# A 528-column product finishes its first 264 columns before it starts the second

## The reference

```python
def hybrid_layer(x, norm_g, w_in, q_norm_g, k_norm_g, rpb, w_o_attn, w_o_na, w_out, cos, sin):
    h = rms_norm_2(x, norm_g)
    proj = jnp.einsum('bld,de->ble', h, w_in)
    qa, ka, va, za, qb, kb, vb, zb, ga, gb = split_cols(proj)
...
    ya = jnp.einsum('ble,ed->bld', oa, w_o_attn)
    yb = jnp.einsum('ble,ed->bld', ob, w_o_na)
    mixed = jax.nn.sigmoid(ga) * ya + jax.nn.sigmoid(gb) * yb
    return x + jnp.einsum('bld,de->ble', mixed, w_out)
```

## Time and profile before

| | |
|---|---|
| median of 3 runs | 1615.57 us (1615.27 to 1616.48) |
| the profiled execution | 1616.05 us |
| its span, first to last instruction | 1614.8 us |
| mean granted TensorE clock | 0.994 |
| PE, PEld, DVE, ACT busy | 96%, 83%, 55%, 39% |
| line 581 (all matmuls of `pe_terms`) on the chain that ended last | 69% of the span |

### The profile page before, as it was taken

How to read it: one execution, slowest core, us unless ns; L and a number is a source line. 1 busy time by engine, 2 the same in 40 slices (tenths; PEclk the granted TensorE clock), 3 DMA queues, 4 the chain that set the end, 5 groups by cost and what they waited for, 6 DMA issues and landing times.

```text
span 1614.8 us, 24777 instructions
## 1 busy us (share of the span) xinstructions
PE 1552.9 (96%) x10341; PEld 1333.9 (83%) x10341; DVE 882.8 (55%) x1592; ACT 636.8 (39%) x1134; POOL 48.7 (3%) x50
## 2 busy tenths in 40 slices
PE   7999979999999999999999899999999999999997
PEld 5898866678888888899998788999998987678886
DVE  4435656666645655875554554446664454554443
ACT  5233346543322343744344443223343343542333
POOL 0000001000000000020000000000020000000000
PEclk9999999999999999999999999999999999999999
DMA  6232300033323332432112102224431113013231
GB/s 196 84 83 54 103 14 14 27 106 102 105 86 97 104 103 80 106 72 72 53 53 53 53 23 71 92 79 142 82 79 53 53 53 65 28 40 107 89 118 53
DMA packets 168192, 123.05 MB, mean 76 GB/s; under 512 B 48640, under 2 KB 163840, under 8 KB 168080
## 3 DMA queue, kind: packets, MB, share of 16 engines
q1 hardware_dynamic: 168080, 121.46, 26.4%
HBM read 119.35 MB, written 2.10 MB: 75 GB/s over the span
## 4 chain that ended last, share of the span: by engine, by line
PE 88%; DVE 5%; ACT 4%; issue 2%; POOL 0%; DVEq 0%; ACTq 0%; POOLq 0%
PE bank L581 69%; PE bank L2798 2%; PE bank L2764 2%; PE bank L2778 2%; DVE w_lo L541 1%; PE bank L3174 1%; ACT w_hi L532 1%; PE bank L2668 1%; PE bank L1650 1%; PE bank L1593 1%; PE bank L2619 1%; PE bank L1469 1%; PE bank L3137 1%; PE bank L3153 1%; ACT probs L1523 1%
## 5 line engine op out<-in xcount | busy, mean ns | idle before, releaser
L541 DVE TENSOR_TENSOR w_lo<-w_raw,w_hi 128x2048 fp32r<-128x2048 f32 (+2 forms) x117 | 241.1, 2061 | 167.8 <-ACT w_hi L532 167.2
L581 PE MATMUL bank<-h_hi,w_hi 128*128 128x512 f32 (+2 forms) x920 | 323.6, 372 | 6.0 <-DVE w_lo L541 2.2
L581 PE MATMUL bank<-h_hi,w_lo 128*128 128x512 f32 (+2 forms) x920 | 317.6, 365 | 0.0
L581 PE MATMUL bank<-h_lo,w_hi 128*128 128x512 f32 (+2 forms) x920 | 317.3, 365 | 0.0
L532 ACT ACTIVATE w_hi<-w_raw 128x2048 fp32r<-128x2048 f32 (+2 forms) x117 | 201.0, 1719 | 64.9 <-DMA w_raw<-w_in 28.9
L581 PEld LDWEIGHTS bank<-h_hi,w_hi 128*128 128x128 f32 (+1 forms) x920 | 165.7, 189 | 42.7 <-issue 12.9
L581 PEld LDWEIGHTS bank<-h_hi,w_lo 128*128 128x128 f32 (+1 forms) x920 | 165.5, 188 | 28.3
L581 PEld LDWEIGHTS bank<-h_lo,w_hi 128*128 128x128 f32 (+1 forms) x920 | 165.6, 188 | 26.7 <-issue 0.5
L581 PE MATMUL bank<-g_hi,w_hi 128*128 128x264 f32 (+1 forms) x752 | 181.3, 307 | 1.5 <-DVE z_a L2217 0.9
L581 PE MATMUL bank<-g_hi,w_lo 128*128 128x264 f32 (+1 forms) x752 | 178.7, 303 | 0.0
L581 PE MATMUL bank<-g_lo,w_hi 128*128 128x264 f32 (+1 forms) x752 | 178.7, 303 | 0.0
(11 more groups left out here) (593 smaller groups left out, 2614.9 us busy)
## 6 DMA issues: line engine op xcount, KB each, us to landing
w_raw<-w_in SPq DMA_DIRECT2D x45, 1024.0 KB, 5.2
w_raw<-w_up SPq DMA_DIRECT2D x32, 512.0 KB, 5.2
w_raw<-w_in SPq DMA_DIRECT2D x40, 256.0 KB, 4.5
w_raw<-w_down SPq DMA_DIRECT2D x8, 1024.0 KB, 5.2
w_raw<-w_out SPq DMA_DIRECT2D x8, 1024.0 KB, 5.1
w_raw<-w_out SPq DMA_DIRECT2D x8, 512.0 KB, 3.4
w_raw<-w_ple_gate SPq DMA_DIRECT2D x4, 1024.0 KB, 5.0
w_raw<-w_o_attn SPq DMA_DIRECT2D x8, 512.0 KB, 3.4
```

Of the source, the lines that this page charges most:

```text
L541: DV.e.tensor_tensor(wlo[u % RING][:, 0:n], raw[u % RING][:, 0:n], whi[u % RING][:, 0:n].bitcast(F32), ALU.subtract).then_inc(*w_low(u))
L581: ins = PE.e.matmul(out, stationary[a](k), moving[b](k)[i], start=first and n == 0, stop=last and n == 2)
```

## The change

In `pe_features` the loop over the two halves moves outside the loop over the input blocks. All blocks of the first half run, then all blocks of the second half. The waits for the activations' marks stay with the first half alone. The semaphore `product` still goes with the last matmul of the whole product. The argument `freed` is given by no caller. Products of 512 columns have one chunk and keep their order.

```diff
         def pe_features(act, kts, w, cols, n, banks, freed=None):
             ch = chunks(n)
-            mv_ = [lambda k, t=t: [t[:, k, a:b] for a, b in ch] for t in act[:2]]
-            for k in range(kts):
-                for mark in act[2](k):
-                    PE.wait_ge(*mark)
-                for c, b0 in zip(cols, banks):
-                    outs = [bank[:, b0 + i, 0:b - a] for i, (a, b) in enumerate(ch)]
-                    ins = pe_terms(outs, [lambda k, t=t, c=c: c(t, k) for t in w[:2]], mv_, k, k == 0, k == kts - 1)
-                if freed and k < kts - 1:
-                    freed(k, ins)
+            for i, (start, stop) in enumerate(ch):
+                for k in range(kts):
+                    for mark in act[2](k) if i == 0 else ():
+                        PE.wait_ge(*mark)
+                    for c, b0 in zip(cols, banks):
+                        ins = pe_terms([bank[:, b0 + i, 0:stop - start]], [lambda k, t=t, c=c: c(t, k) for t in w[:2]],
+                                       [lambda k, t=t: [t[:, k, start:stop]] for t in act[:2]], k, k == 0, k == kts - 1)
+                    if freed and i == len(ch) - 1 and k < kts - 1:
+                        freed(k, ins)
             return ins
```

## The result

The changed kernel takes 1623.25 us (median of 4 runs, 1622.13 to 1624.54) against 1615.88 for the kernel before (4 runs beside them): ratio 1.0046, interval 1.0028 to 1.0063. In a second series (experiment e5) it is 1621.73 against 1616.73 with ratio 1.0033 (1.0021 to 1.0046). The kernel became slower by 5 to 7 us; the forecast was 1616.8 in a range up to 1618.6.

A forecast was written before the change was run, and what follows sets the result against it. TensorE's stream, busy 96% of the span and paced by its weight loads, was taken as the bound. Reordering 0 plus stall and restart 1.23 us on the median 1615.57 gave 1616.8 us, range 1615.0 to 1618.6.

The forecast's parts named there:

- The order of the matmuls: TensorE's 3072 reordered matmuls: number, forms and weight loads stay, distance stays at 0.120 us, cost 0.
- the bounds that I gave: Reordering 3072 matmuls: from 7 us less (0.1177 us each) to 10 us more (0.1232 us each).
- the edge that I named as proof against me: Prediction is wrong if the distance of 264-column matmuls moves by more than 0.001 us.
- rivals with 0.10 of the chance: Reordered matmuls slower, 1626.6 us (chance 0.06), or faster with one bank, 1610 us (0.04); both outside the range.
- Rival 1: All 3072 reordered matmuls: one that doesn't alternate costs more, 0.0032 us each, 10 us; 1626.6 us; chance 0.06.
- the fixed piece: Each matmul costs its columns plus 0.0132 us, taken from the 512- and 256-column streams; hidden until now by alternation.
- The sentence on pairs and weight loads: Skill's rule that weights loaded once serve many matmuls favours pairs; trace shows one load per matmul, so the term is 0.
- The stall: First product of mixed, before its 22nd matmul: TensorE waits 1.11 us for the eighth block, 1.23 us with restart.
- The waits for oa and ob: Products reading oa and ob: low parts are made before the products start, so the earlier waits stay empty.
- No slack behind: TensorE has no wait for 173 us from 987.70, so the 1.23 us delay reaches the end in full.
- The sum: Whole kernel: median 1615.57 us plus 1.23 us gives 1616.8 us, 0.08% more.

The follow-up runs named there:

- e5: The changed kernel again, unedited, in more runs beside new runs of the kernel before; 1621.73 us, ratio 1.0033.
- e9: Changed kernel with halves of 256 columns read from columns 8 and 264, 16 columns left out; 1612.70 us.
- e10: Changed kernel with halves of 272 columns from 0 and 256, 16 columns computed twice; 1637.80 us.
- e11: Kernel before (both halves in each block) with the second half read from columns 256 to 519; 1629.61 us.
- e13: Kernel before with the weight tiles alone moved 32 bytes further on in memory; 1630.29 us.
- e4: Kernel before (both halves in each block) with the first half read from columns 8 to 271; 1626.27 us, ratio 1.0056.
- e2: Changed kernel with second halves read from column 256 instead of 264; 1619.57 us, ratio 1.0020.
- e7: Kernel before with 6 and 28 extra matmuls, results overwritten, at two places (0.72 and 3.36 us); 1620.19 us, ratio 1.0030.
- e6: Changed kernel with the first product of mixed in the old order and second halves read from columns 256 to 519; 1617.03 us, ratio 1.0006.

## Why the prediction was wrong, point by point

**The step that failed** is the first: "The order of the matmuls", with "I take the cost as 0". It rested on "the stream runs at the pace of its weight loads", read from the earlier trace rows: 256 columns in one bank at the same distance as 264 in two, and quicker with narrow weights. Two things were wrong in it. There is no fixed floor: with the same loads, 256 columns ran at 0.1167 (e9), 272 at 0.1254 (e10) and paired 264 at 0.1233 (e11), and the gain of narrow weights turns into a loss when the weights lie 32 bytes further on (0.1186 against 0.1167, e13). Whether it is the load or the stream of columns that takes longer at another place, no run shows. And the two streams compared differed in more than their banks: the earlier trace rows has columns and weights that both start at the same place, has a half that starts 32 bytes off in every pair. So their near equality, 0.1199 and 0.1200, was no evidence of a common floor; why several streams stand at 0.1200 isn't shown. The cost measured is 0.0010 for each of 3072 matmuls, 3.2 us. It lay inside the bounds that I gave (-7 to +10) and at the edge that I named as proof against me (0.001), but the range did not reach to it, since I kept the bounds to rivals with 0.10 of the chance.

**Rival 1** had the direction right, and that an un-alternated matmul costs more. What must take turns is neither the bank nor the use of one weight block, as it supposed: the pairs of e4 and e11 alternate between two banks on the same weights and stand at 0.1225 and 0.1233. It is two places of the columns against the weights. Its size, 0.0032, was three times too large: the fixed piece behind it isn't one, as a start moved by 32 bytes changes what is left over (0.1200 and 0.1167 for the same 256 columns).

**The sentence on pairs and weight loads** was weighed rightly: pairs save no load (10341 and 10341 before and after), and e11 shows that pairs can be slower than single halves (0.1233 against 0.1205 in e2 with the same columns).

**The stall** was right in place, matmul, releaser and nearly in size: 1.23 predicted with the restart, 1.5 and 1.3 us measured with it in two profiles. In the first, the eighth block was ready 1110.16 - 1106.37 = 3.79 us after the product's start instead of 3.63, and the wait's end to the matmul took 0.15 instead of 0.04. What it got wrong is why the block can't be ready sooner: not by the ob product alone, since VectorE comes to the blocks of mixed straight from the split of w_out (L541), and that hangs on a transfer. So the stall's size varies with a transfer, in which the prediction, with "The chain has no share of a DMA", saw no part. The waits for oa and ob stayed empty: the products from 990.20 to the stall follow each other without a gap. No slack behind took the stall back: the work added in e7, 3.36 us of it in the next product, reached the end in full.

**The sum** of the two lasting terms is 3.2 + 1.3 to 1.5 = 4.5 to 4.7 us, or 1620.1 to 1620.3; the two series say 1621.7 and 1623.3 with intervals of +3.4 to +7.4 and +4.5 to +10.2 us. The profile of e5, which has no fall at the two places, lost 4.3 to 4.4 us from the first changed product on. Undoing both terms gives the time of before (e6). The rest of the medians, half a microsecond in the one series and 3 us in the other, isn't settled: falls of the clock, for which the prediction had no term, account for 3.1 us in the one profile, they come and go, and whether the new order makes them more frequent was not shown.

## What to carry to other kernels

When a stream of matmuls waits for nothing and yet is slower than its columns, don't name a floor from two streams that happen to agree; vary length and start by one step each and see what moves. Where columns are cut into pieces, look at where each piece starts against the weights it is multiplied by: 32 bytes were worth 3% at 512 and at 256 columns, with opposite signs. A loop turned inside out also moves every wait in it forward; find the one source that is made block by block just ahead, count the matmuls to its last block, and see what the engine that makes it was doing before.

## What the hardware showed that I had not expected

The distance between these matmuls changes with the place of the moving columns against that of the weights: at 512 columns 0.2267 us at the same place and 0.2333 with the weights 32 or 64 bytes on, 0.2343 with 96; at 256 columns 0.1200 at the same place and 0.1167 with the columns 32 bytes on. A cut at column 264 of a row puts the second half 32 bytes off.

At 264 columns one kind of place does not have one pace. Products with the same places run at 0.1200 or at 0.1213 throughout, and two halves that alternate between two places run at 0.1200, quicker than either kind alone when alternated with itself (0.1225 and 0.1233). It depends on what went before, too (mixed at 0.1213 behind a stall in e2, at 0.1200 without one in e6). What sets the pace within a product, and why the sign turns between 256 and 512 columns, stays open.

The granted clock fell to 0.59 and 0.57 in stretches of 4 us from 907 and from 1191 in one profile of the changed kernel and stayed at 1.00 there in another, with the same instructions in the same order.
